# Four edits to a two-block kernel on one core: small loads, a norm by halves, fewer columns, experts summed in PSUM

## The reference, cut to what matters

```
# block 1, layer 0: mix = conformer_conv(x); layer 1: mix = diff_attention(x)
def conformer_conv(x, ...):
    a, gate = split(x @ w_pw1 + b_pw1);  h = a * sigmoid(gate)
    h = depthwise_conv(h, 31 taps) + b_dw
    return silu(layer_norm(h, g, b)) @ w_pw2 + b_pw2
x = layer_norm(ALPHA * x + mix, ...)                    # ALPHA = 4 ** 0.25
out = sum over 16 experts: gate_e * ((silu(x@wg_e) * (x@wu_e)) @ wd_e)   # two experts per token
x = layer_norm(ALPHA * x + out, ...)                    # LN_EPS = 1e-5

# block 2: 16 meta tokens in front of the 256, so L = 272
z, xbc, dt, q, k, v = split(rms_norm(h) @ w_in)
y_ssd = rms_norm(ssd(xbc, dt) * silu(z));  y_sb = rms_norm(stick_breaking(q, k, v))
h = h + rms_norm(concat(y_ssd, y_sb) @ w_out)
g = causal_dwconv(x @ w_up_gate, 3 taps);  h = h + rms_norm((gelu(g) * u) @ w_down)
return h[:, 16:]                                        # the meta tokens are dropped
```

## Time and profile before

| | before |
|---|---|
| median of 3 runs | 1486.72 us (1485.76 to 1489.68) |
| the profiled execution, its own time | 1485.41 us |
| its span | 1483.70 us |
| PE busy | 1357.4 us, 91% of the span |
| DVE, ACT, POOL busy | 384.4, 263.2, 24.6 us |
| mean granted clock of PE | 0.946 of full speed |

### The profile page before, as it was taken

One profiled execution on the slowest core, in us unless ns is written; L12 is line 12 of the kernel. 1 busy time (PEld: TensorE's weight loads), 2 busy tenths in 40 slices (PEclk: granted clock), 3 DMA queues, 4 the chain that ended last, 5 costly groups with the idle time before them and its releaser, 6 DMA issues.

```text
span 1483.7 us, 15495 instructions
## 1 busy us (share of the span) xinstructions
PE 1357.4 (91%) x6438; PEld 852.5 (57%) x6438; DVE 384.4 (26%) x857; ACT 263.2 (18%) x565; POOL 24.6 (2%) x49
## 2 busy tenths in 40 slices
PE   7979799999989978799999969988899996999997
PEld 6744434444347754434444358866686785888743
DVE  0013512112141332521112141465303205222201
ACT  1002311001102331311001121321325103000000
POOL 3110000000000000000000000000000000000000
PEclk9989799999999987799999979988999998999998
DMA  9960699999961050699999941311221033543420
GB/s 327 315 173 1 255 380 426 425 426 427 402 234 57 24 204 1 255 391 427 425 425 427 401 167 56 115 57 57 85 86 57 0 114 115 169 161 127 167 85 28
DMA packets 91663, 314.36 MB, mean 212 GB/s; under 512 B 9746, under 2 KB 47158, under 8 KB 77766
## 3 DMA queue, kind: packets, MB, share of 16 engines
q1 hardware_dynamic: 77344, 298.98, 52.0%
q10 hardware_dynamic: 14246, 14.33, 3.4%
HBM read 311.05 MB, written 2.24 MB: 211 GB/s over the span
## 4 chain that ended last, share of the span: by engine, by line
PE 88%; DVE 7%; DMA 1%; issue 1%; ACTq 1%; ACT 1%; DVEq 0%; SPq 0%; POOLq 0%
PE psum L243 37%; PE psum L1460 15%; PE psum L1493 8%; PE psum L681 6%; PE psum L2676 5%; PE psum L561 4%; PE psum L1505 4%; PE psum L462 1%; PE psum L859 1%; PE psum L1636 1%; PE psum L1634 1%; DMA ring<-in_a_w_pw 1%; PE psum L2334 1%; PE psum L2326 1%; PE psum L2321 1%
## 5 line engine op out<-in xcount | busy, mean ns | idle before, releaser
L243 PE MATMUL psum<-xT,ring 128*128 128x256 f32 (+2 forms) x1792 | 413.0, 392 | 8.8 <-POOLq L442 5.2
L243 PEld LDWEIGHTS psum<-xT,ring 128*128 128x128 f32 x1792 | 346.0, 194 | 72.4 <-issue 15.3
L1460 PE MATMUL psum<-ring,arena 128*64 128x512 f32 x768 | 169.6, 594 | 0.0
L1460 PEld LDWEIGHTS psum<-ring,arena 128*64 128x64 f32 x768 | 53.9, 137 | 103.9 <-issue 103.7
L243 PE MATMUL psum<-arena 128*128 128x128 f32 (+4 forms) x684 | 92.4, 291 | 1.2 <-issue 1.1
L243 PEld LDWEIGHTS psum<-arena 128*128 128x128 f32 (+2 forms) x684 | 84.1, 198 | 5.5 <-issue 4.8
L1493 PE MATMUL psum<-ring,arena 128*64 128x512 f32 x384 | 85.0, 595 | 0.0
L1365 DVE TENSOR_TENSOR arena<-psum,arena 64x512 f32<-64x512 f32 x32 | 34.3, 1073 | 191.5 <-ACT arena L1413 191.5
L2676 PE MATMUL psum<-ring,arena 128*128 128x512 f32 x176 | 75.7, 592 | 0.0
L1413 ACT ACTIVATE arena<-psum 64x512 f32<-64x512 f32 x32 | 18.9, 592 | 259.4 <-PE psum L1460 259.4
L561 PE MATMUL psum<-ring,arena 128*128 128x512 f32 x128 | 60.3, 632 | 4.5 <-ACT arena L1000 3.6
(11 more groups left out here) (319 smaller groups left out, 1184.4 us busy)
## 6 DMA issues: line engine op xcount, KB each, us to landing
ring<-in_moe_w_gate SPq DMA_DIRECT2D x24, 2048.0 KB, 11.8
ring<-in_moe_w_up SPq DMA_DIRECT2D x24, 2048.0 KB, 15.9
ring<-in_moe_w_down SPq DMA_DIRECT2D x24, 2048.0 KB, 16.1
ring<-in_w_in SPq DMA_DIRECT2D x11, 2048.0 KB, 13.6
ring<-in_w_up SPq DMA_DIRECT2D x22, 1024.0 KB, 7.7
arena<-in_moe_w_gate SPq DMA_DIRECT2D x8, 2048.0 KB, 12.2
ring<-in_w_down SPq DMA_DIRECT2D x5, 2048.0 KB, 7.7
ring<-in_a_w_pw SPq DMA_DIRECT2D x8, 1024.0 KB, 10.9
```

Of the source, the lines that this page charges most:

```text
L243: last = nc.tensor.matmul(dst, lhsT, rhs, start=(n == 0), stop=(n == len(pairs) - 1))
L1460: last = pe.matmul(bank(j)[part, :], tokens[:, k, side * SEATS:side * SEATS + SEATS], weights(u + n, k), start=(k == 0), stop=(k == KC - 1))
```

## The change

Six places are touched.

1. **Small loads.** The sixteen loads leave ACT's list. SP issues them on the weights' queue just ahead of the `pw2` blocks; in front of the second of them SP waits for the constants made by POOL.
2. **Conv norm by token halves.** Reciprocal, subtraction, product and SiLU go over tokens 0 to 127 for all chunks, then over 128 to 255. PE's first half waits for the first eight SiLUs, its second half for the others.
3. **258 tokens.** `NEED = 14`: gate z, queries, the output projection and some small meta-token operations work on columns 14 to 271. ACT zeroes the 14 unused columns of each turned result once.
4. **Experts on top of x.** PE writes x into banks 4 to 7 by an identity matmul (four of 128x512) between the router's logits and the seat counts. The gates carry a factor 1/ALPHA, the norm uses LN_EPS/ALPHA**2, and the statistics and the normalization read PSUM. ACT's scaling of x, DVE's clearing of the banks and the four additions in `ffn_norm` go.
5. **Pair order.** Pair 0 fetches the next tokens before its turn. The last pair scatters two of the four sums, turns, then scatters the other two.
6. **Last scatter.** Its four matmuls go by column half, and each half waits only for its own copy out of PSUM.

```diff
             if u == unit_at["pw2"]:
+                sp.dma_start(b_pw2, a["a_b_pw2"][0].partition_broadcast(P)).then_inc(bias_rows_loaded, 16)
+                sp.wait_ge(consts_made, CONSTS_MADE)
+                sp.dma_start(router_w[:, :, 0:EXPERTS], ...).then_inc(inputs_loaded, 16)
...
+                load_norm(0, a["ln_mix_g"][0], a["ln_mix_b"][0], sp)
             slot_freed(u)
...
-            dve_step(dve.tensor_tensor(conv[:, 0, :], conv[:, 0, :], mean_b, ALU.subtract))
-            reciprocal_of(dve, rstd_b, root)
-            dve.tensor_tensor(conv[:, 0, :], conv[:, 0, :], rstd_b, ALU.mult).then_inc(conv_normed, 1)
...
+            for c in range(2):
+                centre(0, c)
+            dve.wait_ge(std_ready, root)
+            for t in range(2):
+                cols = slice(t * P, t * P + P)
+                dve_step(dve.reciprocal(rstd_b[:, cols], rstd_b[:, cols]))
+                for c in range(KC):
+                    if t or c >= 2:
+                        centre(t, c)
+                    dve.tensor_tensor(conv[:, c, cols], conv[:, c, cols], rstd_b[:, cols], ALU.mult).then_inc(
+                        conv_normed, 1)
...
-                        last = nc.tensor.matmul(bank(first + c)[:, 0:L],
+                        last = nc.tensor.matmul(bank(first + c)[:, NEED:L],
                                                 slot_k(part_units[half])[:, k, (c % 4) * P:(c % 4) * P + P],
-                                                src[:, k, :], start=(i == 0 and k == 0),
+                                                src[:, k, NEED:L], start=(i == 0 and k == 0),
...
-            act.activation(x_nat[:, 1:3, :], x_nat[:, 1:3, :], ACT.Copy, scale=ALPHA).then_inc(rows_ready, 1)
...
+            for t in (1, 2):
+                pe.wait_ge(normed[2 * layer], 2 + t)
+                for half in range(2):
+                    pe.matmul(psum[:, BANKS + 2 * t - 2 + half, :], ident[:, :], x_nat[:, t, half * 512:half * 512 + 512],
+                              start=True, stop=False, skip_group_check=True)
             take_bank(J + 2)
...
-            experts_sum(layer, 1, 0)
-            experts_sum(layer, 1, 1)
-            variance_of(k, 1)
-            experts_sum(layer, 2, 0)
...
+            experts_stats(layer, 1, 0)
+            experts_stats(layer, 2, 0)
+            experts_stats(layer, 1, 1)
+            variance_of(k, 1, 3)
+            experts_stats(layer, 2, 1)
+            variance_of(k, 2, 4)
...
-            dve.memset(psum[:, BANKS:2 * BANKS, :], 0.0).then_inc(cleared, 1)
...
+                if p == 0:
+                    fetch_next(p)
+                    turn(p)
+                elif p < LAST:
+                    scatter(p - 1, TOP + LOWER)
+                    turn(p)
+                    fetch_next(p)
+                else:
+                    scatter(p - 1, TOP)
+                    turn(p)
+                    scatter(p - 1, LOWER)
                 down(p)
-            scatter(LAST)
+            scatter(LAST, ((0, 0), (1, 0), (0, 1), (1, 1)))
```

More of the change, by code:

```diff
@@ L558, in part @@
             for k in range(KC):
-                if ready is not None and j == first:
-                    ready(k)
+                if ready is not None and half == 0:
+                    ready(k, t)
                 last = pe.matmul(bank(j), lhs(k, t), slot_k(u0 + half)[:, k, :], start=(k == 0), stop=(k == KC - 1))
@@ L2598, in _ @@
         def _(pe):
[L2600 removed]
+            products(psum[:, BANKS, NEED:L], [(ones[:, :], sqT[:, c, NEED:L]) for c in range(KC)]).then_inc(so_summed, 1)
             w = unit_at["w_out"]
```

235 lines of the change are left out of this document (115 added, 120 removed).

## The result

| | before | after |
|---|---|---|
| median on one chip | 1486.84 us (4 runs) | 1452.53 us (4 runs, 1446.25 to 1455.60) |
| all runs, with those beside the experiments | 1487.45 us (51 runs) | 1450.6 us (14 runs, 1446.25 to 1456.19) |
| profiled execution, its own time | 1485.41 us | 1455.60 us |
| mean granted clock (47 and 14 runs) | 0.942 | 0.959 |

The first comparison gave a ratio of 0.9761 (95% interval 0.9723 to 0.9799). The forecast was 27.1 us. The profiled executions differ by 29.8 us.

A forecast was written before the change was run, and what follows sets the result against it. PE, busy 91% of the span, was taken as the bound. Terms 9.6 + 1.1 + 3.0 + 2.0 + 3.5 + 2.6 + 0 + 5.3 = 27.1 us took 1485.4 to 1458.3, plus 1.3 for the median: 1459.6 us, range 1452 to 1470.

The forecast's parts named there:

- Small loads: Convolution: squares start 9.9 us earlier, less 1.5 us backlog, plus 1.2 us clock; 9.6 us gained (3 to 11.5).
- backlog: Convolution: moved loads delay chunk transfers, taken as 1.5 us; bounds 0 and 5 for the write alone, 7 if taps wait.
- rival A: Convolution: backlog makes taps or the last chunk wait, small-loads term only 3.6 us, 1465.6 us in all; chance 0.14.
- Conv norm by halves: Gap ahead of the first SiLU: shorter reciprocal, product and SiLU gain 1.1 us; up to 2.6 us of clock not counted.
- Identity matmuls: Routing gap: matmuls end about 1.3 us late but the fetch runs faster; 1.5 us per layer, 3.0 in all.
- rival B: Routing: clock stays low, each layer loses 2.7 us instead of gaining 1.5, 1468.0 us in all; chance 0.10.
- First pair: Experts' first pair: fetch covers the 1.87 us wait, a 0.89 us wait shows; net 1.0 us per layer, 2.0.
- Last pair and last scatter: Experts' end: reordered work hides waits of 0.89 and 0.88 us; 1.75 us per layer, 3.5 (2.8 to 3.7).
- Norm after the experts: Layer 1's gap falls from 10.12 to 7.5 us, 2.6 gained; layer 0's 3.65 us stays, 0 gained.
- 258 columns: Fourteen fewer columns: output projection 2.9, gate z 1.5, queries 0.5 and 0.4; 5.3 us (4.3 to 6.0).
- Rival C: Experts become bound by their weights, the 5.5 us saved by pairs returns as waits, 1465.1 us; chance 0.05.
- Rival D: Shorter gaps spare more clock, 2.6 us in the norm and 1.5 more per routing layer, 1454 us; chance 0.06.

The follow-up runs named there:

- e4: Changed kernel with thirteen of the sixteen small loads issued late by SP, after the fourth expert block, when DMA engines are idle: 1444.32 us against 1486.41 before.
- e1: Kernel before with only the sixteen small loads moved from ACT's list to SP's, ahead of pw2: 1477.64 against 1486.41 us.
- e14: Changed kernel plus one DVE copy of 704 columns in the norm after layer 0's experts: 1453.43 us against 1487.89 before.
- e7: Kernel before with only the new order of pairs and of the last scatter, sums still started from cleared banks: 1475.28 against 1486.82 us.
- e9: e4 plus 28 dummy matmuls in PE's gap between layer 1's last scatter and the second block's transposes: 1445.82 us against 1488.31 before.
- e10: e9 plus dummy matmuls in five more kinds of gap, among them the attention's last six heads: 1442.34 us against 1488.31 before.
- e16: e10 with fewer dummy matmuls in the two longest gaps and eight ahead of the second projection: 1436.35 us against 1487.89 before.
- e15: Changed kernel plus eight dummy matmuls in the gap ahead of the second projection: 1451.56 us against 1487.89 before.
- e13: Changed kernel plus two redundant DVE copies ahead of the conv norm's first reciprocal, making the gap 3.24 us: 1454.58 us against 1487.89 before.
- e11: e4 plus one DVE copy of 1024 columns in the norm after layer 1's experts: 1446.78 us against 1488.31 before.

## Why the prediction was wrong

The steps, each by the profiled pair (forecast, measured):

- **Small loads** 9.6, measured 8.7: 6.7 us to the first squares and 2.0 of clock in the norm. The backlog was taken as 1.5 us. Against e4 it delayed the squares by 4.2 us and left PE idle for 5.0, the upper bound given for the write alone, and it hit two chunks' taps too, which was rival A's sign. That the term still came out near is luck: without the backlog the squares would have been 10.9 us earlier and not 9.9 (e4), and the clock gave 2.0 us and not 1.2. The rule of the Trainium skill from "DMA: Bandwidth & Descriptors", "Issuing engines are not separate DMA queues", holds in so far as the transfers stayed on the same engines and slowed the chunks. What it makes of this edit, no gain, does not agree with e1: 10.4 us of issuing were on the path, and the edit gained 8.8 us.
- **Conv norm by halves** 1.1, and its gap measured 1.04. But the kernel without it is 9 us slower, twice, and on the kernel before it alone gained 5.8 us. The clock that this term put at nothing ("I count none") is what was mis-sized.
- **Identity matmuls** 3.0, measured 1.3 and 1.3. At half rate they took 6.66 us, which was rival B's sign, but the fetch is fast again, as described, so B's loss did not come. The seat counts start 1.7 us late and not 1.3 (7.34 us behind L1187, 5.64 us behind L1173 before).
- **First pair** 2.0, measured 0.98 and 0.97.
- **Last pair and last scatter** 3.5, measured 0.67 and 0.66 for the turn, 0.28 in layer 0 and 0.88 in layer 1 for the scatter: 2.5. In layer 0 the wait ahead of the scatter went, but PE's list held the transposes (e14; in e7 the profile gives "issue" for 4.30 us there, no engine), so 0.6 of the 0.88 us came back as gap.
- **Norm after the experts** 2.6, measured 2.9 in layer 1 (10.12 to 7.26). In layer 0 that PE's list bound was right. The estimate after the Trainium skill, "VectorE: DVE Perf Modes", "Why PSUM operands drop a tier", was 1.2 us for a row of 1024 read from PSUM, and L576 takes 1.34 (0.81 before from SBUF), hidden. The row operation with two tensor inputs is not slower from PSUM: L649 takes 1.28 us, and its counterpart of before, L613, took 1.28 from SBUF.
- **258 columns** 5.3, measured 6.3 of work: 2.0 in z, 1.2 in queries and small operations, 3.0 in the output projection.

These are 26.0 us, against 27.1. Rival C did not come: layer 0's experts hold 228.4 us of work and 5.2 us of idle PE (7.3 before), so no wait for weights was added. The pair differs by 29.8: the other 3.9 us are clock in stages whose work is the same (attention 3.3 and two neighbours 0.7 us worse, state-space part 4.3, stick-breaking 1.7, gate z 1.6, turned rows 0.4 better).

**The step that failed** is the clock. The prediction counted half clock behind two gaps only, the norm's and routing's, put what the halves spare at nothing, and took the loss of all other stages as given. It then turned one execution into the median by adding the 1.3 us between them. The runs showed 29.8 us between the profiled executions, and more between medians: in the first comparison 1.4 us because the profile of before was faster than its median and 3.1 us because that of after was slower than its own, 34.3 us in all; over all runs 2.0 and 5.0 us, 36.9 us in all. Against the 26.0 us of the terms that leaves 8 to 11 us that no term holds. The mean clock went from 0.942 to 0.959, and the loss from 47.9 us to 43.1, 37.3 and 36.8 us in the three profiles of the changed kernel. Rival D named the mechanism, shorter gaps spare clock, but limited it to 5.6 us in two stages and gave it 0.06. The loss of before, 48 us, could be read from its trace, and I gave a range to that of two stages only.

**What stays open.** That idle time of PE brings the half clock on for what stands behind it, and that work in the gap takes it away, is shown for the transposes and the attention (e9, e10, e16). Why the kernel without the halves is 9 us slower in ten of ten runs, mostly in stages 300 to 1000 us later, is not, and so the cause of those 8 to 11 us is argued and not shown. The gap's length does not settle it: e15 closes it and gains nothing, e13 makes it longer and stays within the noise. Nor do single executions, since one kernel shows several values (8.7, 9.8 or 12.1 us in the attention). A shift of later stages against the moments at which the clock steps would fit, but e14 shifted nothing and e11 is inconclusive.

## What to carry to other kernels

Cut a trace into work at full rate, half-clock loss and idle before you sum a change, and give the loss a range of its own: here it was 48 us, and the change lowered it by 5 to 11 us, according to the execution. Take a profile of more than one execution before a forecast hangs on one, since two of the same kernel differed by 7 us. A load that can be issued when the queues are empty should wait for that moment: moving it off a busy engine gained 8.8 us, moving it out of busy DMA engines 4 to 6 more.

## What the runs showed of the hardware

- Gains of single edits were larger than their own work and waits: 8.8 + 8.8 + 5.8 + 8.3 + 11.5 = 43 us alone, 37 together, where the named terms hold 26.
- Dummy matmuls paid: 34 us of them, in gaps, made the kernel 8 us faster (e16 against e4) by lifting the mean granted clock from 0.962 to 0.982.
- Behind the last scatter PE could issue nothing for 3 to 4 us (3.09 in e9, 4.00 in e10), however much work stood in its list; in layer 0 such a stretch hid a copy of 0.84 us on DVE (e14).
- Sixteen small loads ahead of 2 MB blocks kept SP issuing for 18.8 us (from 23.2 to 42.0). The blocks behind them then held 94.8% of the DMA engines at 70 to 80 us (26.4% in e4), and a chunk of the convolution took 13.34 us to DRAM (7.41 before).
